# A blocked triangular inverse that carries R = (1+N)T and its transpose along, in the chunked delta rule of a hybrid decoder layer

## What is computed

```python
def wkv7_scan(s0, r, w, k, v, a, b):
    def step(s, inp):
        r_t, w_t, k_t, v_t, a_t, b_t = inp
        sa = jnp.einsum('bhij,bhj->bhi', s, a_t)
        s = s * w_t[:, :, None, :] + sa[..., :, None] * b_t[..., None, :] + v_t[..., :, None] * k_t[..., None, :]
        y = jnp.einsum('bhij,bhj->bhi', s, r_t)
        return s, y
```

## Time and profile before

| what | us |
|---|---|
| runs | 1100.80, 1099.84, 1094.39 |
| median | 1099.84 |
| span of the profiled execution, first to last instruction | 1095.3 |
| of it `phase_inputs` | 217.7 |
| `phase_chunks` | 199.7 |
| `phase_gating` to the end | 677.9 |

### The profile page before, as it was taken

How to read it: one execution, slowest core, us unless ns; L and a number is a source line. 1 busy time by engine, 2 the same in 40 slices (tenths; PEclk the granted TensorE clock), 3 DMA queues, 4 the chain that set the end, 5 groups by cost and what they waited for, 6 DMA issues and landing times. The chain is left out here.

```text
span 1095.3 us, 24864 instructions
## 1 busy us (share of the span) xinstructions
PE 1020.0 (93%) x10457; PEld 766.3 (70%) x10457; DVE 562.5 (51%) x1194; ACT 371.1 (34%) x796; POOL 442.2 (40%) x459
## 2 busy tenths in 40 slices
PE   5999999799999899999999999999997999997886
PEld 5777778588888887888888788885464555554442
DVE  6577777656555553777654546333365322221225
ACT  3444545545555443444325452000112111110113
POOL 7646646245455423878573334440001122221110
PEclk9999999999999999999999999999999999998998
DMA  8022221030000006641034224233969999999996
GB/s 262 11 75 75 82 83 39 2 85 4 4 5 4 4 4 161 196 115 39 16 95 148 77 77 154 77 115 134 418 258 380 385 415 414 414 417 416 411 378 234
DMA packets 86008, 182.99 MB, mean 167 GB/s; under 512 B 9897, under 2 KB 59589, under 8 KB 78218
## 3 DMA queue, kind: packets, MB, share of 16 engines
q1 hardware_dynamic: 79325, 168.59, 42.4%
q0 software_dynamic: 5088, 8.43, 2.1%
q10 hardware_dynamic: 1485, 4.39, 1.0%
HBM read 172.98 MB, written 17.55 MB: 174 GB/s over the span
## 5 line engine op out<-in xcount | busy, mean ns | idle before, releaser
L2324 POOL DMA_INDIRECT d_y<-tl_xn,ex_sidx x32 | 32.0, 1000 | 110.9 <-DVE tl_xn L2916 103.2
L2912 DVE SCALAR_TENSOR_TENSOR ex_sg<-tl_psA,ex_slot_rs,ex_sg 128x128 f32<-128x128 f32 x32 | 11.2, 351 | 123.1 <-ACT ex_sg L2683 122.9
L2319 POOL DMA_INDIRECT tl_xn<-d_tok,ex_gidx x16 | 16.8, 1050 | 141.5 <-DVEq L2907 78.2
L264 PE MATMUL psv<-xT,w_sum 128*128 128x260 f32 x256 | 61.5, 383 | 0.8 <-DVE uv_gu L1597 0.6
L226 POOL TENSOR_TENSOR w_sum<-w 128x512 f32<-128x512 f32 x16 | 21.1, 1322 | 94.1 <-PE mg_w L264 93.9
L264 PEld LDWEIGHTS psv<-xT,w_sum 128*128 128x128 f32 x256 | 48.5, 190 | 9.0 <-issue 1.0
L2683 ACT ACTIVATE ex_sg<-tl_psA,ex_slot_rs 128x128 f32<-128x128 f32 x32 | 11.7, 367 | 121.9 <-PE tl_psA L2517 121.9
L1060 PE MATMUL ck_b<-ck_X,ck_V 64*64 64x64 f32 x1280 | 50.1, 222 | 2.7 <-issue 1.6
L264 PE MATMUL rk_ps<-xT,rk_w 128*128 128x260 f32 x208 | 50.1, 384 | 0.0
L264 PE MATMUL rk_ps<-xS,rk_w 128*128 128x260 f32 x200 | 48.6, 386 | 0.0
L1060 PEld LDWEIGHTS ck_b<-ck_X,ck_V 64*64 64x64 f32 x1280 | 43.1, 134 | 4.3 <-issue 4.1
(11 more groups left out here) (645 smaller groups left out, 2802.8 us busy)
## 6 DMA issues: line engine op xcount, KB each, us to landing
wd<-in_moe_w_down SPq DMA_DIRECT2D x13, 1024.0 KB, 23.1
rk_w<-in_w_in SPq DMA_DIRECT2D x12, 1024.0 KB, 5.5
w_uv<-in_w_in SPq DMA_DIRECT2D x16, 512.0 KB, 5.3
w<-in_w_in SPq DMA_DIRECT2D x8, 1024.0 KB, 5.9
tl_x<-in_moe_w_down SPq DMA_DIRECT2D x8, 1024.0 KB, 19.1
xT<-in_moe_w_gate SPq DMA_DIRECT2D x5, 1024.0 KB
xT<-in_moe_w_up SPq DMA_DIRECT2D x5, 1024.0 KB
w<-in_proj_a SPq DMA_DIRECT2D x4, 1024.0 KB, 5.0
```

Source lines behind the costliest of these rows:

```text
L264: ins = eng.matmul(bank[:, 0:TH], w[:, k, :], x[:, k, :], start=(first and k == 0), stop=(last and k == NK // 2 - 1), skip_group_check=True)
L2319: eng.indirect_dma_start(out=xg[:, p % 2, :], out_offset=None, in_=m.d_tok, in_offset=bass.IndirectOffsetOnAxis(ap=gidx[:, p:p + 1], axis= ...
L2324: eng.indirect_dma_start(out=m.d_y2, out_offset=bass.IndirectOffsetOnAxis(ap=rows, axis=0), in_=yo[:, x, :], in_offset=None, bounds_check= ...
L2912: eng.scalar_tensor_tensor(out=sg[:, out, :], in0=psg[out][:, P:2 * P], scalar=scale, in1=sg[:, out, :], op0=ALU.mult, op1=ALU.mult).then_ ...
```

## The change

Instead of X, Z and nb the kernel carries one tile XQ with, for each head, X = T of the diagonal blocks and Q, which is (1+N)T turned, side by side. With V the masked R = (1+N)T of the level, T' = T V and Q' = Q V in effect, so a level is two matmuls a head that depend on the same two evictions: R' from Q and V (L1063), 64 columns, and [X', Q'] from V and XQ (L1073), one matmul with 128 moving columns. The last two levels need only X' (L1075), the last one no R'. VectorE evicts R' with the mask of the next level, ScalarE evicts XQ in one operation. `turn_x` and its eviction are gone; V of the start comes from a VectorE transpose in blocks of 32x32 (L1234), and two products for each head are made once ahead of the levels (`first_products`, L1045, L1049).

Half of the pairs (t = 1) change halves: their matmuls read `lo` and write `hi` or the other way round, while those of the other half (t = 0) stay in their own half. The order inside a group is lo->lo, hi->hi, lo->hi, hi->lo. The outputs of t = 0 and t = 1 lie in two PSUM banks (`RB[g]`, `XB[g]`), and one eviction reads both.

Further moves: levels run group by group; `old_rhs` and `old_y` stand ahead of each group's level 2 and 3 products; the decay of the state moves from VectorE to GpSimd (`decayed`, L1317), behind GpSimd's X of the next chunk; y is added by VectorE after both state additions; all evictions of v move to ScalarE.

```diff
-            def level(c, lv):
-                for g in range(G):
-                    if lv == 0:
-                        eng.wait_ge(s_z1[g], c + 1)
-                        eng.wait_ge(s_lk[g], 2 * c + 2)
+            def level(c, lv, g):
+                eng.wait_ge(s_x_e[g], c * NX + lv + 1)
+                if lv == 2:
+                    old_rhs(c, g)
+                if lv == 3:
+                    old_y(c, g)
+                eng.wait_ge(s_w_e[g], c * NL + lv + 1)
+                V = Vs[(lv + 1) % 2]
+                if lv < NL - 1:
+                    for t, n, p, own, other in heads(g):
+                        at, to = rows_at(t, lv, own, other), rows_at(t, lv + 1, own, other)
+                        last = eng.matmul(out_r(g, t, n)[to], XQ[at, p, 1, :], V[at, p, :], start=True, stop=True)
+                    last.then_inc(s_w[g], 1)
...
+                    if lv < NL - 2:
+                        last = eng.matmul(out_xq(g, t, n)[to], V[at, p, :], XQ[at, p, :, :], start=True, stop=True)
...
                 for g in range(G):
-                    turn_x(c, g)
-                for g in range(G):
                     turn_bk(c, g)
                 for g in range(G):
                     turn_v(c, g)
+                for g in range(G):
+                    first_products(c, g)
                 for lv in range(NL):
-                    level(c, lv)
+                    for g in range(G):
+                        level(c, lv, g)
...
                 for g in range(G):
                     new_state(c, g)
+                for g in range(G):
+                    new_y(c, g)
                 if c + 1 < NC:
+                    turned(c + 1, 0)
                     masked_k(c + 1, 1, hi, 0)
+                    turned(c + 1, 1)
                     masked_k(c + 1, 1, lo, 1)
...
+            def decayed(c, g):
+                eng.wait_ge(s_sa[g], c + 1)
+                eng.tensor_tensor(st[:, grp(g), :], st[:, grp(g), :],
+                                  running(c, CH, CH + 1)[:, grp(g), :].to_broadcast([P, GP, HD]), ALU.mult).then_inc(s_st[g], 1)
...
                 for g in range(G):
                     with_diagonal(c + 1, g)
-                eng.wait_ge(s_x1[1], c + 2)
+                for g in range(G):
+                    decayed(c, g)
...
+            for g in range(G):
+                decayed(NC - 1, g)
             for g in range(G):
                 eng.wait_ge(s_s0[g], 2 * NC)
```

More of the change, by code:

```diff
@@ L1027, in turn_v @@
                     eng.wait_ge(s_sv_e, 1)
-                for n, p, own, other in heads(g):
-                    last = eng.matmul(b64(b[3])[other, n, :], m.v[own, p, tokens(c)], m.ident[own, own], start=True, stop=True)
+                for n in range(GP):
+                    for own, other in ((lo, hi), (hi, lo)):
+                        last = eng.matmul(b64(XB[g][:, 1])[other, n, :], m.v[own, g * GP + n, tokens(c)], m.ident[own, own],
+                                          start=True, stop=True)
@@ L1030, in turn_v @@
                 last.then_inc(s_tb[g], 1)
-            def level(c, lv):
-                for g in range(G):
-                    if lv == 0:
-                        eng.wait_ge(s_z1[g], c + 1)
-                        eng.wait_ge(s_lk[g], 2 * c + 2)
-                    else:
[L1039 to L1043, removed]
-                for g in range(G):
[L1045 to L1062, removed]
-                    new_x.then_inc(s_x[g], 1)
@@ L1065, in old_rhs, with old_y @@
             def old_rhs(c, g):
                 eng.wait_ge(s_s0[g], c * 2 + 2)
+                for t, n, p, own, other in heads(g):
+                    which = 0 if own == lo else 1
+                    last = eng.matmul(b64(XB[g][:, 0], GP * HD)[rows_at(t, 1, own, other), t * HP + n, :], L[:, p, which, 0:CH],
+                                      wv[:, p, which, :], start=True, stop=True)
+                last.then_inc(s_rhs[g], 1)
+            def old_y(c, g):
                 for n in range(GP):
@@ L1079, in old_y @@
+                    last = eng.matmul(b64(XB[g][:, 1], GP * HD)[hi, n, :], wv[:, p, 1, :], L[:, p, 1, CH:P], start=True, stop=True)
                 last.then_inc(s_ry[g], 1)
             def corrected(c, g):
[L1082 to L1085 removed]
+                eng.wait_ge(s_rh_e[g], 2 * c + 2)
@@ L1086, in corrected @@
+                eng.wait_ge(s_x_e[g], c * NX + NX)
+                for t, n, p, own, other in heads(g):
+                    at = rows_at(t, 1, own, other)
+                    last = eng.matmul(out_u(g, t, n)[own], XQ[at, p, 0, :], rh[at, p, :], start=True, stop=True)
                 last.then_inc(s_u[g], 1)
```

211 lines of the change are left out of this document (112 added, 99 removed).

## The result

The changed kernel takes 1066.6 us (median, 1064.34 to 1068.75) where the one before took 1100.32 beside it: ratio 0.972, 95% interval 0.968 to 0.975. A later comparison of the same two kernels, with more runs of the one before, gave 1069.36 against 1096.35 us: 0.975 [0.973, 0.976]. The profiled spans differ by 29.2 us (1095.3 and 1066.1).

The account below looks back on a forecast made before the run. TensorE, busy 92 to 94% but waiting on evictions within levels, was taken as the bound. Savings of 19.5 + 2.6 + 1.7 + 2.5 = 26.3 us, less slip 24, gave 1099.8 - 24 = 1076 us; 80% range 1067 to 1090.

Parts of the forecast that it names:

- its walk: Operation-by-operation schedule of one chunk, each instruction at its earliest start: period 20.5 us instead of 23.75.
- S to F: From the start of the next chunk's scores (S) to its inverse's first product (F): 7.1 us instead of 8.8.
- F to the next S: From the inverse's first product, through its levels, to the next chunk's scores: 13.4 us with a handover.
- both clocks: TensorE's levels with their evictions, and GpSimd's six operations behind the exponential: both were to end at F + 13.3.
- VectorE's second product of L: VectorE's other part of L, after level 3's old_y and ahead of evicting R: F + 11.5 to 12.2, 0.68 us.
- the first stage: First level of chunk 0 to the scores of chunk 1, 15.25 us before: F 0.8 earlier, then 13.4; 2.6 saved.
- the allowance for slip: Taken off the summed saving for handovers that slip: 0.3 us for each of eight chunks, 26.3 to 24.
- the last product: TensorE's product at the phase's end, held some 2 us by weight sums: F + 19.4 to 21.5, 2.5 us saved.
- four tiles don't overlap: Rival, 10%: in the levels, R takes 0.47 and XQ 0.9 us a group; period 23.1, total 1095 us.
- GpSimd's chain: Rival, 14%: its six operations ahead of the scores stretch to 1.72 us each, 10.3 instead of 8.4; total 1087 us.
- The slower rival: Rival, 4%: tiles crossing halves run one after another, 58 ns a 64-column record; period 33.6, total 1180 us.
- the rule weighed there: Trainium skill: different row tiles cannot access one PSUM bank simultaneously; by it the new levels would run at half rate.

Follow-up runs that it names:

- The kernel without crossing: Changed kernel, but every pair stays in its own half (lo->lo, hi->hi only): 1095.07 us, ratio to the kernel before 0.999 [0.997, 1.001].
- the early exponentials: Changed kernel with the next chunk's two exponentials first in ScalarE's chunk, GpSimd's products also waiting for its last X: 1061.01, again 1061.81 us.

## Why the prediction was right, and where it was off

**Right, by the steps of its walk.** S to F: 7.1 forecast, 6.93 in the window, 7.02 on average. F to the next S: 13.4 forecast, 13.36 from F at 266.64 to S at 280.00, 13.26 on average. Along it the exponential at F + 4.2 (4.17), the second eviction pair behind it at 5.5 (5.37), level 2 at 6.15 (6.00), GpSimd from 4.9 to 13.3 (4.87 to 13.30), and both clocks meeting at the scores. 16 records of [X, Q] took 0.43 us, forecast 0.45. `turned`, whose duration had no row, takes 0.43 us (forecast 0.42), and holds nothing up.

**Right in part by luck.** VectorE's second product of L was put at 0.68 us from F + 11.5; it began at F + 11.07 and took 1.10, so two errors of 0.4 us cancel. In the first stage F was to come 0.8 us earlier and came 0.24 earlier, while the rest took 13.03 us and not 13.4, which cancels again.

**Off: the allowance for slip.** The sum was 26.3 us, less 0.3 us for each of eight chunks, 24. Hardly any such slip shows; one of the six periods has a wait of 0.71 us for nothing that the profile shows. Within the phase the terms measured are six periods 20.8 (forecast 19.5), the first stage 15.25 + 0.24 for the earlier F less 13.03, so 2.5 (2.6), the last S to F 1.9 (1.7), and from the last F to the end of the last product 24.0 less 21.1, so 2.9 (2.5); 28.0 in all. The periods are 0.2 us shorter than the walk, which took 0.2 to 0.3 us of tail before every reader. Taking off a slip on top of a walk that had its handovers in it already counted them twice; that is 2.4 of the 4 us missing in the phase. The 20.8 also hold some scatter of the kernel before, whose last two periods were 24.93 and 24.61 us in its profile, with waits of 0.24 to 0.61 us for nothing that it shows, and the other four 23.0 to 23.4.

**Off: the last product.** The weight sums were to hold TensorE up by some 2 us.

```profile
384.56 1.92 PE L264 MATMUL psv<-xT,w_uv 128*128 128x260 f32 x8
385.56 1.69 POOL L1358 TENSOR_TENSOR t_first<-w_uv 128x128 f32<-128x128 f32 x4
387.30 2.02 PE L264 MATMUL psv<-xS,t_first 128*128 128x260 f32 x8 [0.82 <-POOL t_first L1358]
```

They do, by 0.82 us. GpSimd's queue was right, since the product starts at F + 19.1 (forecast 19.4); too short was TensorE's own work ahead of it, done at F + 18.3 where the 2 us put it at 17.4. The product ends at F + 21.1, forecast 21.5.

**Off: from span to median.** The forecast took a saving on the span off the median of the runs shown, 1099.8. The runs before scatter over 7.5 us, and their medians in the later calls were 1096.4 to 1097.7. In every run whose span is on record the time is 1.7 to 1.8 us above it, so the execution with the span of 1095.3 took about 1097.0 (an estimate), and the rest of the 4.5 us was scatter of the runs. With the later medians the measured saving is 27 us in the direct comparison (1096.35 to 1069.36), near the 28.0 of the phase; the 33.7 us of the first comparison contain the scatter of four runs. The 9.4 us by which the first median lies below 1076 are thus 4 of saving in the phase that was not counted, 2.8 from 1099.8 to 1097.0, 1.3 by which the profiled run (1067.86) lies above its median, and 1.2 of the span's difference outside the phase. These lie mostly behind it, where TensorE has the lower clock for 29.6 us of the profile before and for 23.1 of the profile after; that this is the cause is not shown.

**The rivals.** That four tiles don't overlap is false of the changed kernel. The kernel without crossing is that rival, and its period was priced well, 23.3 us for 23.1. That the time is its 1095 us as well is chance: the rival took 5 us off 1099.8, and this kernel is 1.4 us below the one before in the same call, an interval that holds zero. GpSimd's chain did not stretch: its operations took 1.26, 1.26, 1.27, 1.72, 1.28 and 1.71 us. The slower rival needed 32 ns a record of 64 columns; 16 in 0.28 us are 17.5. And the rule weighed there, that row tiles can't be at one bank at once, is refuted in this form by the changed kernel itself: lo->lo and hi->hi write one bank in different partitions, and beside the crossing pair they run at that rate. The Trainium skill has another page that fits these rows (PSUM — Partial Sum Buffer, PSUM bank collisions raise a hardware error): it also quotes the wider rule, but for what was measured it puts the collision, of two row tiles of TensorE too, at the same bank and the same quadrant, that is the same 32 partitions. By that rule, this trace agrees: lo->lo and hi->hi are in different quadrants. What it says of two row tiles that write the same quadrant of a bank no run here shows; the kernel keeps lo->lo and hi->lo in two banks.

## What to carry to other kernels

Count the 64x64 matmuls per tile of the array, not per engine: a group's time was that of its busiest tile (0.12 to 0.14 us a matmul of 64 columns), so in the levels the algebra with fewer, larger steps paid only when half of the work was sent across halves; TensorE was busy for 99% of the time without that, for 88% with it. When a change shortens the engine that bounds, list what runs beside it with its slack in us (1.4 here on GpSimd): a slack smaller than the gain is the next bound, and then moving the head of that chain, which was worth nothing before, is worth 6 to 7 us. And a walk that has every handover in it needs no further allowance.

## What the runs showed of the hardware

The order of matmuls among tiles matters much less than their balance: eight matmuls of which the four for one pair of tiles come first and the four for the other pair behind them took 0.28 us, as when all four tiles alternate.

At the lower clock level (granted 0.50) two records of the scores, 128 columns each, stand at 0.43 us in the trace, where they stand at 0.28 at the higher one.

VectorE's and GpSimd's products with both operands in SBUF lengthen one another, and in these rows it is the one that starts while the other is under way that pays. In the changed kernel VectorE starts at 274.92 and 277.71 into a GpSimd product and takes 0.97 and 1.10 us, and each time GpSimd's next one starts into VectorE's and takes 1.72 and 1.71, while the GpSimd product that was first keeps its 1.27 and 1.28. With the early exponentials VectorE is first by 0.04 us:

```profile
272.02 0.68 DVE L989 TENSOR_TENSOR ck_L<-kk_all,spare 64x512 f32<-64x512 f32 x1 [2.28 <-PE ck_x L1082]
```

It keeps 0.68 us, and GpSimd, at 272.06, takes 1.80. That the two share their way into SBUF for VectorE's instructions with two SBUF inputs is stated by the Trainium skill (GPSIMD Engine Reference, Specifications); this trace agrees.

A transpose of 128x256 in blocks of 32x32 between two tiles in SBUF costs VectorE 0.43 to 0.45 us, about as much as a product of that shape that reads PSUM (0.41).
